# One core, two model blocks: retention merged with its output step, earlier weight loads, and down weights on ScalarE's queue

## What is computed

```python
mx = split(silu(c) @ w_mod[l] + b_mod[l], 6)          # modulation, first thing in a layer
# retention, per head, chunks of 128 tokens, forward and backward
a = (q @ k.T) * intra                                 # intra = exp(distance * log_gamma)
y = a @ v + (q @ state) * q_dec
state = state * c_dec + (k * k_dec).T @ v
# retention_output, per head of 64
mu = mean(y, -1); var = mean((y - mu) ** 2, -1)
out = silu(gate) * ((y - mu) * rsqrt(var + EPS)) * gn_g
# experts: 4 groups of 8, the best group, two experts in it
for g in range(N_GROUPS):
    m = silu(t @ w_gate[g]) * (t @ w_up[g]) * combine[g]
    y = y + m @ w_down[g]
```

## Time and profile before

| | |
|---|---|
| runs | 3098.82 us median of 3, 3098.35 to 3103.83 |
| profiled execution | 3099.36 us, of which the span is 3096.7 |
| TensorE clock over the span | 0.904 of full |
| PE busy | 2595.7 us, 84% |
| DVE, ACT, POOL busy | 1450.3, 812.0, 228.5 us |
| DMA | 323.87 MB, mean 105 GB/s |

### The profile page before, as it was taken

The page is one execution under the profiler, slowest core; times in us unless marked ns, Lnnn a source line. Parts: engine busy times, 40 slices in busy tenths (PEclk is TensorE's granted clock), DMA queues, the critical chain, the costliest instruction groups (busy, mean ns, idle before and its releaser), DMA issues. The chain is left out here.

```text
span 3096.7 us, 34950 instructions
## 1 busy us (share of the span) xinstructions
PE 2595.7 (84%) x14622; PEld 1971.8 (64%) x14622; DVE 1450.3 (47%) x2278; ACT 812.0 (26%) x1300; POOL 228.5 (7%) x162
## 2 busy tenths in 40 slices
PE   6996884999998998995589998977885976987886
PEld 4884543888887787983479996724632355764332
DVE  3225226376666424326547774254476536332223
ACT  3222322143232313223233333132301423221001
POOL 0004301000000000006200000000011000011111
PEclk9997967999999999998789998968886987987998
DMA  5112940111211111221012221310201013227996
GB/s 215 55 62 100 364 171 1 55 55 55 69 55 56 47 66 64 69 93 41 5 69 82 96 88 66 106 60 28 78 1 35 1 41 106 85 116 317 424 425 264
DMA packets 52108, 323.87 MB, mean 105 GB/s; under 512 B 7341, under 2 KB 13613, under 8 KB 24109
## 3 DMA queue, kind: packets, MB, share of 16 engines
q1 hardware_dynamic: 38016, 289.97, 24.9%
q10 hardware_dynamic: 8286, 19.06, 1.7%
q0 software_dynamic: 5648, 12.59, 1.1%
HBM read 317.39 MB, written 12.58 MB: 107 GB/s over the span
## 5 line engine op out<-in xcount | busy, mean ns | idle before, releaser
L774 PE MATMUL ps<-work_rounded,ring_rounded 128*128 128x512 f32 (+2 forms) x2544 | 675.3, 359 | 13.9 <-DVE work_rounded L391 13.6
L1721 PE MATMUL ps<-xn_rounded,ring_rounded 128*128 128x258 f32 (+2 forms) x2816 | 535.5, 312 | 0.0
L774 PE MATMUL ps<-xn_rounded,ring_rounded 128*128 128x512 f32 (+1 forms) x2112 | 499.6, 344 | 12.9 <-DVE xn_rounded L618 12.9
L774 PEld LDWEIGHTS ps<-work_rounded,ring_rounded 128*128 128x128 f32 (+1 forms) x2544 | 435.4, 193 | 89.8 <-issue 15.2
L1721 PEld LDWEIGHTS ps<-xn_rounded,ring_rounded 128*128 128x128 f32 x2816 | 415.2, 191 | 31.3
L774 PE MATMUL ps<-big_rounded,ring_rounded 128*128 128x512 f32 (+2 forms) x936 | 307.0, 370 | 112.0 <-DVE big_rounded L618 102.8
L774 PEld LDWEIGHTS ps<-xn_rounded,ring_rounded 128*128 128x128 f32 x2112 | 339.3, 192 | 62.8 <-DVE xn_rounded L618 13.7
L1721 PE MATMUL ps<-work_rounded,ring_rounded 128*128 128x256 f32 (+1 forms) x1232 | 281.7, 310 | 13.8 <-DVE work_rounded L391 9.5
L618 DVE TENSOR_TENSOR ring_rounded<-ring,ring_rounded 128x2048 fp32r<-128x2048 f32 (+1 forms) x86 | 173.4, 2018 | 208.6 <-ACT ring_rounded L596 208.6
L596 ACT ACTIVATE ring_rounded<-ring 128x2048 fp32r<-128x2048 f32 (+1 forms) x86 | 145.3, 1691 | 474.3 <-PE ps L774 401.2
L774 PEld LDWEIGHTS ps<-big_rounded,ring_rounded 128*128 128x128 f32 (+1 forms) x936 | 164.8, 194 | 148.5 <-DVE ring_rounded L618 87.1
(11 more groups left out here) (336 smaller groups left out, 3149.1 us busy)
## 6 DMA issues: line engine op xcount, KB each, us to landing
ring<-in_stream SPq DMA_DIRECT2D x149, 1024.0 KB, 4.8
big<-in_experts SPq DMA_DIRECT2D x22, 2048.0 KB, 29.5
ring<-in_stream SPq DMA_DIRECT2D x32, 704.0 KB, 3.8
ring<-in_experts SPq DMA_DIRECT2D x22, 1024.0 KB, 30.0
xn<-in_experts SPq DMA_DIRECT2D x5, 2048.0 KB, 30.6
work<-in_experts SPq DMA_DIRECT2D x5, 2048.0 KB, 35.7
work<-in_bias ACTq DMA_DIRECT2D x24, 256.0 KB, 3.4
xn<-in_experts SPq DMA_DIRECT2D x5, 1024.0 KB, 32.9
```

What stands on the lines that cost most here:

```text
L774: mm = pe.matmul(out[:, a - u.first:b - u.first], lhs, rhs, start=j == 0 and n == 0, stop=j == terms - 1 and n == len(passes) - 1)
L1721: mm = pe.matmul(out[:, a:b], ws[:, k, :], x[k][:, a - base:b - base], start=k == 0 and n == 0, stop=k == KT - 1 and n == 2)
```

## The change

- **Start.** The 8 strips of the first modulation leave the ring and get places in `big`. They are issued first on SP's queue, then one ring strip, then the tokens (moved from ACT's queue), then two ring strips. Two PSUM areas alternate for the products, and the sum of strip n-1 comes behind the products of strip n.
- **Retention.** The ramp is loaded one stage earlier. ACT builds the two factors of the mask with 12 exponentials, POOL multiplies them; DVE's 12 instructions for the argument go. `retention_output` is gone: the mean is removed beforehand, since the values of retention are multiplied by (identity - group matrix) where `pooling` turned them; the gate's Silu sits in `pooling`; squares, variance, root and gate run inside the retention stage, pair by pair. The reciprocal square root becomes Ln and then Exp on ACT.
- **Experts.** `gu` 0 and 4 and `dn` 4 are loaded beside the memory attention, `gu` 1 and 2 beside the projection, and `dn` 0 to 3, `gu` 3 and `dn` 5 beside routing. The first two gathers are issued in the routing stage. All later `dn` loads are issued from ACT's queue, behind the Silu of each pair. The results come back as four transfers, one for each 128 tokens.

```diff
-    plan += modulation[:MOD_FIRST]
+        self.partial_ps = [b.bank(0, 256), b.bank(1, 256)] if resident else [bank[:, 0:256]]
...
+        if n >= 1 and self.resident:
+            self.sum(pe, n - 1)
... start
+                for i, (area, strip_landed) in enumerate(self.first_modulation):
+                    sp.dma_start(area, self.t["first_modulation"][i]).then_inc(strip_landed, 16)
+                self.load_strips(sp, 1)
+                sp.dma_start(self.h, self.t["tokens"]).then_inc(self.sig("tokens_landed").up(16), 16)
                 self.load_strips(sp)
-                act.dma_start(self.h, self.t["tokens"]).then_inc(self.sig("tokens_landed").up(16), 16)
... pooling
+                for i in range(3):
+                    act.activation(px[:, GATE + i, 0:gate_width], px[:, GATE + i, 0:gate_width], ACT.Silu)
+                        for p in range(3):
+                            mm = pe.matmul(self.bank(4 + n % 4)[:, p * P:(p + 1) * P], px[:, tile + p, a:a + P], centring, start=True, stop=True)
... retention, TensorE
                 for p in range(3):
-                    values(p)
                     if p + 1 < 3:
                         scores(p + 1)
+                    values(p)
+                    if p >= 1:
+                        variances(p - 1)
+                variances(2)
... retention, ScalarE
-                act.activation(mask, arg, ACT.Exp).then_inc(powered.up(), 1)
+                for d, (name, distance) in enumerate((("decay_f", fwd), ("decay_b", bwd))):
+                    for h in range(HEADS):
+                        ins = act.activation(factors[d][:, h, :], distance, ACT.Exp, scale=self.v((name, l), h))
+                def square(p):
+                    act.wait_ge(stored.sem, stored.at(p + 1))
+                    if p >= 2:
+                        act.wait_ge(varied.sem, varied.at(p - 1))
+                    act.activation(sq[p % 2][:, 0:qw], px[:, RQ + p, 0:qw], ACT.Square).then_inc(squared.up(), 1)
+                def root(p):
+                    act.wait_ge(varied.sem, varied.at(p + 1))
+                    if p >= 2:
+                        act.wait_ge(gated.sem, gated.at(p - 1))
+                    settle(act, act.activation(rstd[p % 2][:, 0:qw], var, ACT.Ln, bias=EPS), logged)
+                    act.activation(rstd[p % 2][:, 0:qw], rstd[p % 2][:, 0:qw], ACT.Exp, scale=-0.5).then_inc(rooted.up(), 1)
+                square(0)
+                square(1)
+                root(0)
+                square(2)
+                root(1)
+                root(2)
... retention, VectorE
+                weigh(0)
+                weigh(1)
+                store(0)
+                weigh(2)
+                store(1)
+                gate(0)
                 store(2)
-    def retention_output(self, l, need_ctx):
+                gate(1)
+                gate(2)
... routing
+            @block.gpsimd
+            def _(pool):
+                pool.wait_ge(stored.sem, stored.at(16))
+                pool.wait_ge(slotted.sem, slotted.at(1))
+                self.sparse.gather(pool, 0)
+                self.sparse.gather(pool, 1)
... experts, SyncE
         self.load_gu(sp, 5)
-        self.load_dn(sp, 5)
         for n in range(3, self.pairs):
             sp.wait_ge(self.up_done, n - 2)
             for e in range(2):
                 self.load_gu(sp, 2 * n + e)
-            sp.wait_ge(self.down_done, n - 2)
-            for e in range(2):
-                self.load_dn(sp, 2 * n + e)
... experts, ScalarE
             act.activation(self.silu_t, b.bank(2)[:, 0:256], ACT.Silu, scale=b.slot_scale[:, 0, n:n + 1]).then_inc(self.silued, 1)
+            if n + 3 < self.pairs:
+                act.wait_ge(self.down_done, n + 1)
+                for e in range(2):
+                    self.load_dn(act, 2 * (n + 3) + e)
```

More of the change, by code:

```diff
@@ L300, in lay_out @@
     out["stream"] = stream
+    out["first_modulation"] = np.stack([pack_strip(x["w_mod"][0], np.arange(D), np.arange(c, c + 256)) for c in range(0, 256 * MOD_FIRST, 256)])
     experts = np.empty((EXPERTS, P, 3 * STRIP), np.float32)
@@ L456, in products @@
         b = self.b
-        strip = b.strip(pe, len(b.freed_at))
-        if n >= 1:
+        if self.resident:
+            area, landed = self.resident[n]
+            pe.wait_ge(landed, 16)
+            strip = area
+        else:
+            strip = b.strip(pe, len(b.freed_at))
+        if n >= 1 and not self.resident:
             self.sum(pe, n - 1)
@@ L545, in __init__ @@
         self.freed_at = []
+        self.ramp, self.ramp_landed = self.work[:, 9728:10370], nc.alloc_semaphore("ramp_landed")
         self.landed = [nc.alloc_semaphore(f"strip_landed_{i}") for i in range(RING)]
@@ L1003, in start @@
         zeroed = self.sig("zeroed")
+        self.first_modulation = [(self.big[:, i * STRIP:(i + 1) * STRIP], self.nc.alloc_semaphore(f"first_modulation_landed_{i}")) for i in range(MOD_FIRST)]
         with self.stage() as block:
@@ L1365, in context_attention, with load_ramp @@
             outs=lambda h: [px[rows(h), NAQ + h // 2, S:T]],
-            scale=HEAD ** -0.5, tmp=self.work)
+            scale=HEAD ** -0.5, tmp=self.work, prefetch=self.load_ramp)
+    def load_ramp(self, sp):
+        sp.dma_start(self.ramp, self.t["ramp"]).then_inc(self.ramp_landed, 16)
     def retention(self, l, need_ctx):
@@ L1380, in take @@
             return a.rearrange(f"p ({' '.join(letters)}) -> p {' '.join(letters)}", **dict(zip(letters, dims))) if len(dims) > 1 else a
-        table = take(642)
+        table = self.ramp
         fwd, bwd, diag, qramp = table[:, 0:P], table[:, P:2 * P], table[:, 2 * P:3 * P], (table[:, 3 * P:4 * P], table[:, 4 * P:5 * P])
         kramp = (table[:, 640:641], table[:, 641:642])
-        at[0] = 644
         mask, qtab = take(HEADS, P), take(2, 3, P)
         kd, cd = take(2, HEADS), take(2, 3)
-        at[0] = 2208
+        at[0] = 1560
         state = take(2, 5, 192)
-        aw = [take(T) for _ in range(2)]
         qd = [[take(T) for _ in range(2)] for _ in range(2)]
-        arg = aw[0].rearrange("p (h i) -> p h i", h=HEADS)
         kt = [[take(384) for _ in range(2)] for _ in range(2)]
-        assert at[0] <= 10616
+        aw = [[take(T) for _ in range(2)], [px[:, NAV + i, :] for i in range(2)]]
+        assert at[0] <= 9728
+        sq, rstd = [px[:, NAK + i, :] for i in range(2)], [px[:, NAK + 2, :], px[:, NAV + 2, :]]
+        factors = [px[:, RV + i, :].rearrange("p (h i) -> p h i", h=HEADS) for i in range(2)]
         qw = T if need_ctx else S
         order = [4, 5, 0, 3, 1, 2]
-        landed, vstep, argued = self.sig("inputs_landed"), self.sig("vector_step"), self.sig("argued")
+        landed, vstep = self.sig("inputs_landed"), self.sig("vector_step")
         powered, masked, scored = self.sig("powered"), self.sig("masked"), self.sig("scored")
@@ L1557, in _, with weigh @@
                     settle(dve, ins, carried)
-                dve.wait_ge(masked.sem, masked.at(1))
+                dve.wait_ge(masked.sem, masked.at(2))
+                def weigh(p):
+                    dve.wait_ge(scored.sem, scored.at(p + 1))
+                    if p >= 2:
+                        dve.wait_ge(valued.sem, valued.at(p - 1))
+                    for hh in range(2):
+                        h = 2 * p + hh
+                        m = mask[:, h, :].unsqueeze(1)
+                        ins = dve.scalar_tensor_tensor(out=aw[p % 2][hh][:, 0:S].rearrange("p (c i) -> p c i", c=4),
+                                                       in0=sps[hh].rearrange("p (c i) -> p c i", c=4), scalar=HEAD ** -0.5,
+                                                       in1=m.to_broadcast([P, 4, P]), op0=ALU.mult, op1=ALU.mult)
+                        if need_ctx:
+                            ins = dve.scalar_tensor_tensor(out=aw[p % 2][hh][:, S:T].rearrange("p (c i) -> p c i", c=2),
+                                                           in0=cps[hh].rearrange("p (c i) -> p c i", c=2), scalar=HEAD ** -0.5,
+                                                           in1=m.to_broadcast([P, 2, P]), op0=ALU.mult, op1=ALU.mult)
+                        ins.then_inc(weighed.up(), 1)
                 def store(p):
@@ L2713, in gpsimd @@
     def gpsimd(self, pool):
+        for gathered in self.b.sparse.gathered:
+            pool.wait_ge(gathered, 16)
         pool.wait_ge(self.down_done, self.turns * 8)
@@ L2755, in load_dn, with load_beside_attention, load_beside_projection, load_beside_routing @@
         sp.dma_start(self.dn_at[e % 6], self.b.t["experts"][e, :, 4096:6144]).then_inc(self.dn_landed[e % 6], 16)
-    def load_early(self, sp):
-        for e in range(3):
-            self.load_gu(sp, e)
-    def load_first(self, sp):
+    def load_beside_attention(self, sp):
+        self.load_gu(sp, 0)
+        self.load_gu(sp, 4)
+        self.load_dn(sp, 4)
+    def load_beside_projection(self, sp):
+        self.load_gu(sp, 1)
+        self.load_gu(sp, 2)
```

(3 more changed lines are left out.)

201 lines of the change are left out of this document (77 added, 124 removed).

## The result

The changed kernel takes 3048.35 us in the median of 4 runs (3044.99 to 3054.13), beside 3100.3 us for the kernel before in the same session: the ratio is 0.9835, 95% interval 0.9818 to 0.9853, or 52 us less. The profiled execution has a span of 3043.9 us for one of 3096.7. The forecast was 3041.

What follows compares the result with a forecast made beforehand. It saw TensorE unfed at the start's strips and in retention, and the experts bound by DMA. Gains of 6.7 + 25.8 + 16.1 + 9.0 = 57.6 us, from 3098.8, gave 3041; range 3026 to 3060.

Steps and rivals of the forecast that it cites:

- Start: First modulation strips: copies hidden behind products, so the next stage begins at 36.2 instead of 42.97; 6.7 us.
- The second limit: Start: tokens land behind nine strips on one queue, 13.5 MB at 424 GB/s, at 34.3 us, just under 36.2.
- Retention, layer 0: Merged retention and output step: next stage at 511.2 instead of 537.03, ScalarE's chain ending it; 25.8 us.
- Retention, layer 1: The same steps at width 512: next stage at 1533.0 instead of 1549.13; 16.1 us in the sum.
- At nothing: Gates' Silu and values' products in pooling, and earlier expert loads, are hidden under waits or matrix products; 0 us.
- Experts and end: Expert stage: first refill 8.9 us sooner, about 1.4 lost, 1.5 won by results in four parts; 9.0 us.
- order of the last weights: Expert loop: queues taken by turns, packet by packet, bring the last gate and up weights later; costs about 1.4 us.
- gathers become the bound: Rival, expert loop: gathers beside two loaded queues may take 24 us and bind; total gain 46, 3053; chance 0.10 mildly, 0.02 badly.
- Down weights ahead: Rival, expert loop: equal bytes to both queues bring down weights early; total gain 52, 3047 us; chance 0.18.
- Table loads fall away: Rival, retention: one ScalarE table set for Ln and Exp saves loads; gain 72, 3026 us; chance 0.03.
- Handoffs: Rival, merged retention: 20 semaphore steps each cost 0.5 us more; total gain 40, 3059 us; chance 0.09.

Runs made afterwards that it cites:

- e5: The kernel before with the new start alone (resident strips, two product areas, tokens behind nine strips on SyncE's queue); ratio 0.9972.
- e1: The changed kernel run again without any edit, in a second session; 3053.58 us, ratio 0.9865 to the kernel before.
- e6: The kernel before with the merged retention alone (early ramp, factored mask, mean removed beforehand, Silu in pooling, root and gate inside); ratio 0.9846.
- e9: The kernel before with the experts part alone (earlier loads, two early gathers, down weights on ScalarE's queue, results in four parts); ratio 1.0002.
- e2: The changed kernel with the down weights back on SyncE's queue, behind the pair's gate and up weights; 3037.19 us, ratio 0.9800 to the kernel before.
- e10: The kernel before with the experts part alone, but down weights on SyncE's queue; 3084.41 us, ratio 0.9955.
- e3: The changed kernel, both queues kept, with a third buffer for gathered rows, so gathers are issued one pair sooner; 3038.47 us, ratio 0.9804.
- e4: The changed kernel, both queues kept, with each expert weight load issued as two halves of its columns; 3039.64 us, ratio 0.9812.
- e7: As e2, with retention's roots reordered: Ln of second and third pair together, then their Exps, four table loads a layer; 3030.32 us, ratio 0.9791.
- e8: As e7, with all expert weights loaded in halves of their columns on SyncE's queue; 3035.12 us, ratio 0.9798.
- e11: e7 run again without any edit, in another session; 3030.92 us, ratio 0.9786 to the kernel before.

## Why the prediction was right, and where not

The time of 3048.35 lies in the range of 3026 to 3060, and the direction was as forecast. The mark of 3041 was missed by 7 us in one session and 13 in the other. One term, the experts, came out 8.7 us short. In the profile the others, and 2.6 us from stages that the sum put at nothing, made good 3.9 of it: a part of the nearness is luck.

- **Start, 6.7.** Measured 6.2, by another way. The chain of products and copies that gave 36.2 was done by 30.4 here, with five strips of 1.07 us, and by 34.0 in e5, with the 1.93 of the earlier trace rows; it ends the stage in neither. The second limit, the landing of the tokens, set the end at 36.4 + 0.4. The prediction had it at 34.3; it came 2 us later, because it counted only the bytes issued up to the tokens, and 0.9 MB from behind them went with them. The number was near because two limits lay near each other, and that is luck.
- **Retention, layer 0, 25.8.** 25.9 here, 26.3 and 26.5 in e1 and e6. The chain from root 0 on came out step by step, table loads in it. Ahead of it two sizes were off and cancelled: the states end 16.4 us after the stage's beginning and not 15.1, while the first pair's values take 4.3 us and not 6.3.
- **Retention, layer 1, 16.1.** 17.8 here, 18.8 in e1 and in e6. Only a size was off: root 0 ended 30.6 us after the stage's beginning instead of 32.4. What was put too high is decays and states, which end 13.5 us after it and not 15.1; from there to root 0 are 17.1 us for a forecast of 17.3, and the chain behind it holds.
- **At nothing.** Silu and the products for the values in pooling: 0.6 us given back in layer 1 (e6), none of it by a wait for the Silu.
- **Experts and end, 9.0.** This is the step that failed. Refill 7.2 instead of 8.9 sooner (the first rows are turned 5.8 us after the slots are written, not 4.3), last stage 2.2 instead of 1.5, and in between the loop 9.1 longer where the step had 1.4 for the order of the last weights. No run shows those 1.4 us: they stood on an estimate of the author's, from turns by packet between the two queues, and in their place the loop took 9.1 us more. Together 0.3 instead of 9.0, and e9 measures -0.6 by itself. The prediction held that "What the second queue does is order". It also does latency: the rival **gathers become the bound**, given 0.10, is what happened, mildly. e2 and e10 show it by taking the queue away, 11.8 and 13.7 us of loop; e3 by covering the latency, 10.2; e4 by shorter packets, 7.6.
- **Why the rival was priced too low.** It asked whether (9.5 + latency) / 2 would pass the 16.4 us a pair of the bytes, and found the margin at 24 us. At 21.3 us it should not have bound, since that makes 15.4. But 16.4 is the pace of the bytes; the loop before ran ahead on full buffers, 12.6 us a pair at first, and met the landings only later, at 15 to 17. From its first up products (2831.2) to its last (3053.6) it needed 14.8 us a pair, and that is the margin: 15.4 is over it. The changed kernel took 15.7 (2771.1 to 3006.3). With 13 waits of 3 us on average TensorE lost its lead, and at the end stood 11.2 us behind weights that were already there.
- **Down weights ahead, 0.18.** Its mark, no wait for weights between pairs 14 and 15, was seen, but for another reason: TensorE was late. No run tests the order of the two kinds by itself.
- **Table loads fall away, 0.03.** They did not: the changed kernel has six of 1.28 us in each layer. **Handoffs, 0.09.** Not seen.

A second loaded queue raises the gather from 13.6 to 21.0 us (e2, e1), and halved packets on one queue (12555 over the 180 us from 2800 instead of 6411) lower it from 13.5 to 10.1 (e7, e8). That is the direction which turns by packet between the queues would give. The prediction applied turns by packet to the order of the large loads alone, and said that no row showed two loaded hardware queues. The trace of the kernel before has such a stretch, at its start, where the tokens came from ACT's queue (q10) beside the strips of SP's (q1). Between 4 and 18 us:

```profile
q10 hardware_dynamic: 356, 3.44, 57.8%
q1 hardware_dynamic: 345, 2.56, 43.4%
```

Nearly as many packets from each, unlike bytes, and 429 GB/s in all, for 424 with one loaded queue: that fits turns by packet, and the second queue adds next to no bandwidth.

What stays open: why the third to seventh strip take 1.07 us, with a first record of the clock at 16 us, in four executions, and 1.93, with a record only after 46 us, in the others, with the same code and TensorE at work from 12 us on in all of them.

## What to carry to other kernels

Here a second queue for large loads added no bandwidth to transfers that were already full (424 GB/s with one, e2, and with two, e1), and it held up the small transfers on which an engine waited, the gathers, from 13.6 to 21.0 us; before moving a load, look for the short latency-bound transfers that share the engines and price what one more loaded queue makes of them. Cover such a latency (one more buffer) or keep the large loads on one queue: here each won back 10 to 14 us of the loop. And where a change has parts, time them alone: this one was two parts that win and one that does nothing as built, though it wins 14 us with the down weights on the other queue (e10).

## What the hardware showed that was not expected

- A gather of 128 rows of 4 KB took 4.5 us where the queues had just been idle (after, issued at 2763.19; DMA share 0.00 in the 2 us ahead of it and 0.60 until it landed). Medians of all landings that the traces pair, this early one and its like among them: 13.6 us beside one loaded queue with rows of 16 and 8 KB (e2), 10.1 beside one with 8 and 4 KB (e8), 21.3 beside two loaded queues (after), and 28.9 with three buffers beside two (e3, five landings).
- Ahead of a trace's first record of the clock the windows print 1.00. In e5 (first record at 48.1 us, 1.00 printed for 16:46) 16 products took 1.93 us there; in the changed kernel the same ones took 1.07 at a recorded 1.00 (15.8:26.0) and 1.94 at a recorded 0.50 (26.58).
- Halving the rows of the large loads took the rate over 180 us from 424 to 418 GB/s (e1 and e4 with two queues, e7 and e8 with one).
- Transfers queued behind another one were partly carried ahead of its landing, in the start of the changed kernel: 0.9 of the 13.46 MB that SP's queue had moved by 36.4 us, 2.1 us at 424 GB/s.
- One stage, unchanged in all kernels, lasts 132 to 141 us from execution to execution, with a mean granted clock of 0.87 to 0.92. It isn't all of the spread of a kernel's executions, which is 3.5 to 20.7 us here: e7 and e11, the same kernel, differ by 2.8 us in this stage and by 0.2 in their spans.
